# Every ninth weight unit of an expert layer moved as two transfers of 120 and 8 rows

## The reference

```python
for e in range(N_EXPERTS):
    y = y + combine[:, e:e + 1] * swiglu(xt, w_gate[e], w_up[e], w_down[e])
```

## Time and profile before

| | |
|---|---|
| time, median of 3 runs | 1594.76 us (1594.12 to 1596.35) |
| span of the profiled execution, first to last instruction | 1591.7 us |
| TensorE matmuls busy | 1517.8 us, 95% |
| TensorE weight loads busy | 1330.8 us, 84% |
| VectorE busy | 256.7 us, 16% |
| ScalarE busy | 179.0 us, 11% |
| data moved by DMA | 433.48 MB, mean 272 GB/s |
| reads from HBM | 428.89 MB |

### The profile page before, as it was taken

One profiled execution on the slowest core, in us unless ns is written; L12 is line 12 of the kernel. 1 busy time (PEld: TensorE's weight loads), 2 busy tenths in 40 slices (PEclk: granted clock), 3 DMA queues, 4 the chain that ended last, 5 costly groups with the idle time before them and its releaser, 6 DMA issues.

```text
span 1591.7 us, 54543 instructions
## 1 busy us (share of the span) xinstructions
PE 1517.8 (95%) x25973; PEld 1330.8 (84%) x25973; DVE 256.7 (16%) x489; ACT 179.0 (11%) x383; POOL 143.6 (9%) x167
## 2 busy tenths in 40 slices
PE   8999999999999999999999999999999999999997
PEld 7787587777687865989999999899999999998996
DVE  3433310000143435000010010010000000000102
ACT  3233120000131322100000000000000000000001
POOL 2243200000022532200000000000000000000000
PEclk9999999999999999999999999999999999999999
DMA  9213244444242245999999999999999999999992
GB/s 335 89 53 133 106 159 159 159 159 146 92 161 106 76 154 229 360 377 376 363 374 376 357 348 376 356 382 369 365 376 366 370 367 369 367 355 373 389 379 88
DMA packets 133612, 433.48 MB, mean 272 GB/s; under 512 B 9082, under 2 KB 33916, under 8 KB 119052
## 3 DMA queue, kind: packets, MB, share of 16 engines
q1 hardware_dynamic: 132384, 427.70, 71.9%
q0 software_dynamic: 672, 2.14, 0.4%
q10 hardware_dynamic: 332, 0.13, 0.0%
HBM read 428.89 MB, written 1.05 MB: 270 GB/s over the span
## 4 chain that ended last, share of the span: by engine, by line
PE 92%; issue 3%; DVE 2%; ACT 1%; POOL 1%; DMA 0%; ACTq 0%; DVEq 0%
PE ps L1133 35%; PE ps L1157 18%; PE ps L982 9%; PE ps L681 8%; PE ps L993 4%; PE ps L844 4%; PE ps L692 3%; PE ps L1190 2%; PE ps L1062 1%; PE ps L801 1%; PE ps L714 1%; PE ps L677 1%; PE ps L811 1%; PE ps L707 1%; PE ps L821 1%
## 5 line engine op out<-in xcount | busy, mean ns | idle before, releaser
L1157 PE MATMUL ps<-LT_sb,ring 128*64 128x88 f32 x5376 | 218.4, 239 | 16.2 <-issue 15.1
L1157 PEld LDWEIGHTS ps<-LT_sb,ring 128*64 128x64 f32 x5376 | 212.0, 137 | 21.7 <-issue 19.4
L1133 PE MATMUL ps<-wpost,ring 128*64 128x88 f32 x5376 | 217.0, 240 | 12.4 <-issue 10.9
L1133 PE MATMUL ps<-AT_sb,ring 128*64 128x88 f32 x5376 | 217.0, 239 | 9.9 <-issue 9.7
L1133 PEld LDWEIGHTS ps<-wpost,ring 128*64 128x64 f32 x5376 | 210.9, 138 | 17.5 <-issue 15.4
L1133 PEld LDWEIGHTS ps<-AT_sb,ring 128*64 128x64 f32 x5376 | 211.7, 138 | 14.6 <-issue 13.9
L982 PEld LDWEIGHTS ps<-hT_sb,ring 128*128 128x128 f32 x768 | 136.0, 190 | 24.6 <-issue 9.1
L982 PE MATMUL ps<-hT_sb,ring 128*128 128x256 f32 (+1 forms) x768 | 155.7, 362 | 0.0
L681 PE MATMUL ps<-hT_sb,ring 128*128 128x256 f32 x576 | 128.2, 380 | 0.0
L681 PEld LDWEIGHTS ps<-hT_sb,ring 128*128 128x128 f32 x576 | 108.1, 190 | 15.0 <-issue 0.5
L1985 POOL TENSOR_SCALAR small<-small 128x1 f32<-128x1 f32 x16 | 3.9, 241 | 1203.3 <-ACT late L1513 933.6
(11 more groups left out here) (284 smaller groups left out, 1156.5 us busy)
## 6 DMA issues: line engine op xcount, KB each, us to landing
ring<-in_moe_w_gate SPq DMA_DIRECT2D x84, 1024.0 KB, 8.4
ring<-in_moe_w_up SPq DMA_DIRECT2D x84, 1024.0 KB, 8.0
ring<-in_moe_w_down SPq DMA_DIRECT2D x84, 1024.0 KB, 8.2
late<-in_moe_w_up SPq DMA_DIRECT2D x28, 1024.0 KB, 8.5
late<-in_moe_w_gate SPq DMA_DIRECT2D x28, 1024.0 KB, 7.7
late<-in_moe_w_down SPq DMA_DIRECT2D x28, 1024.0 KB, 8.0
ring<-in_ffn_w_gate SPq DMA_DIRECT2D x11, 1024.0 KB, 5.4
ring<-in_ffn_w_up SPq DMA_DIRECT2D x11, 1024.0 KB, 8.1
```

Source lines behind the costliest of these rows:

```text
L1133: ins = mm(o[lo:lo + P // 2, :], pairs[:, m % 2, lo:lo + P // 2], xgT[e % 2][:, k, :], start=(k == 0 and m % 4 == 0), stop=(k == KD - 1), ...
L1157: ins = mm(o[lo:lo + P // 2, :], d[:, i, m * P + lo:m * P + lo + P // 2], moe_hid[:, 2 * j + i, :], start=(first and m % 4 == 0), stop=las ...
```

## The change

Every ninth unit (n mod 9 is 4) is loaded as two transfers, the partitions 0 to 119 and the partitions 120 to 127, into the same buffer and onto the same semaphore. Each of the two adds 16. What TensorE waits for is counted accordingly: 16 for each transfer that the buffer has had up to unit n.

```diff
+CUT_EVERY = 9
+CUTS = (0, 120, P)
+
+def rows_of(n):
+    return list(zip(CUTS, CUTS[1:])) if n % CUT_EVERY == CUT_EVERY // 2 else [(0, P)]
+
+def landings_through(n):
+    return 16 * sum(len(rows_of(m)) for m in range(n % N_UNIT, n + 1, N_UNIT))
...
-                    sp_.dma_start(dst, src).then_inc(unit_landed[n % N_UNIT], 16)
+                    for lo, hi in rows_of(n):
+                        sp_.dma_start(dst[lo:hi], src[lo:hi]).then_inc(unit_landed[n % N_UNIT], 16)
...
-                pe.wait_ge(unit_landed[n % N_UNIT], per_round(r, 16 * (n // N_UNIT + 1), 16 * ROUND_UNITS // N_UNIT))
+                pe.wait_ge(unit_landed[n % N_UNIT], per_round(r, landings_through(n), landings_through(ROUND_UNITS - N_UNIT + n % N_UNIT)))
```

## The result

The changed kernel takes 1714.7 us in the median (1704.23 to 1723.07, 4 runs), against 1594.44 us before (1590.05 to 1596.35, 4 runs): a ratio of 1.0761, 95% interval 1.0717 to 1.0804. It is slower by 120 us, where 28 us less were forecast. The span of the profiled execution is 1712.9 us, 121.2 us longer.

What follows compares the result with a forecast made beforehand. TensorE's matmul stream was taken as the bound, lengthened by 47.3 us of issue gaps from late program blocks. Issue and wait cost nothing; 60% of the gaps, 28 us, was gained: 1594.8 - 28 = 1567 us, range 1550 to 1605.

Steps and rivals of the forecast that it cites:

- What bounds the kernel: Expert layer, from 640 us: TensorE's matmul stream sets the end, lengthened by 47.3 us of issue gaps awaiting late program blocks.
- Program packets all on one engine: Expert layer: assumed all 170 program packets of q8 use one DMA engine, which then moves 23.7 MB against 20.9 MB.
- The sum of 25.9 GB/s: Expert layer: rate of one engine carrying its weights plus all program packets, put against a limit of 24.6 to 25.6 GB/s.
- The argument against evenly spread packets: Expert layer: spread evenly, each engine runs at 23.0 GB/s with 7 to 10% spare, so blocks would seldom be 1.6 us late.
- Bytes per engine: Cut units: 15 engines keep 8 rows each, the spared one loses 2.3 MB, eight engines gain 0.29 MB.
- The gain of 28 us: Expert layer: 60% of the 47.3 us of issue gaps disappears because program blocks arrive earlier on the spared engine.
- The cut transfer is slow: Rival, chance 0.11: cut units load slower, 1614 to 1640 us, or 1595 to 1610 in a milder form.
- 15 engines in each other's way: Milder form of the slow-transfer rival for cut units: the time ends between 1595 and 1610 us.
- 120 rows over 8 engines: Form of the slow-transfer rival: 15 rows per engine, 5.0 us instead of 2.7 per cut unit, 85 us more DMA time.
- third sign of being wrong: Expert layer: TensorE's issue gaps up by 10 us or more, meant to show program packets on one of the eight engines.
- program packets on one of the eight engines: Rival, chance 0.11: the fullest engine gets 0.30 MB more from the 8-row transfers, costing 11.7 us, 1606.5 us.
- SyncE's issue and the wait: Cut units: 37 more DMA starts, 14 us on SyncE but nothing on the path; waiting for 32 increments costs 0.

Runs made afterwards that it cites:

- f2: Kernel before, with the 37 units each loaded as eight transfers of 16 rows, one row on each of 16 engines: 1715.32 us, ratio 1.0778 to the kernel before.

## Why the prediction was wrong

*What bounds the kernel.* Right. TensorE's stream sets the end, issue gaps lengthen it, no matmul waits for a landing, and the gaps end 1.4 us behind a packet of program, in both kernels. The gaps grew when the rate fell.

*Program packets all on one engine.* Not borne out. The step that was looked for between 15 and 16 rows is not there, nor one between 8 and 15 beyond the bytes. The sum of 25.9 GB/s "at or over the limit" rested on this assumption alone and so was no evidence for it. The argument against evenly spread packets took the average load of an engine; that a block can queue behind a burst on any engine, at 23.0 GB/s too, fits the runs and is not shown by itself. Which engines carry the program stays open.

*Bytes per engine, the step that failed.* The count was right: 15 engines and 8, shown by 37 x 7 small packets. The rule for this number in the Trainium skill (DMA: Bandwidth & Descriptors, section Why a DMA increments its semaphore by 16 and not by 1) agrees; that they are the lowest-numbered engines is not shown by any run. What failed was to go from "8 rows each, as before" to the same speed. 8 rows on an engine take 303 ns per 4 KB in place of 164 once the transfer is not of all 128 rows, and what is in flight beside it slows with it.

*The gain of 28 us* therefore lost both of its supports: that the spared engine was the full one did not show, and the transfer that spared it made every packet in flight take nearly twice as long.

*The rivals.* "The cut transfer is slow" had the sign, the place and the test ("the loss per cut unit is over 0.8 us"). I gave it 0.11 and two forms. The form nearest to what was found, 15 engines in each other's way, I had priced at 1595 to 1610 us; it is 1714.7. The other, 120 rows over 8 engines, came near the size by a mechanism that isn't there. The reason that I set against this rival, that 8-row shares are what each engine does now, is the failed step again. A cut unit keeps the rate at half for 6 to 8 us, 1.4 MB (the cut unit and what runs beside it), about 3.5 us of lost engine time, and 121.2/37 = 3.3 us reach the end. That is not because DMA has no time to spare: the copies to HBM were added to the same kernel and cost 1.1 us each for 2.7 us of DMA time. Of the 3.3 us only 81.1/37 = 2.2 are gaps; the rest is the lower clock, which the shorter gaps of the copies did not bring. The prediction's third sign of being wrong, gaps up by 10 us or more, came true, but it was to point at program packets on one of the eight engines, and no run bears that out.

*The clock* was in no term at all. A third of the loss, 42 us, is matmuls at a lower clock. All 21 stretches at 1.2 GHz lie at gaps of 2.4 us and more, and the 101 gaps of up to 1.8 us with the copies of 120 rows brought none; yet 8 gaps of 2.3 to 3.6 us were not followed by one. No run kept TensorE busy through the gaps to show this share alone.

*SyncE's issue and the wait.* The cut by columns, with 37 more starts and the same two-transfer wait, cost about 14 us where nothing was forecast. The starts are not it, at 8 to 10 us for 320 of them, and pieces are smaller in the 11 down units among the 37 only (4 KB in place of 8, which is 11 x 128 = 1408 of the 2000 packets that its page has more; the others are the 592 small ones). What costs the 14 us stays open.

*Why fewer than 128 rows are slow* is settled as to place, not as to mechanism. It is on the write side of on-chip memory, with 15 engines and with 16, from 120 rows down to 16; 112 rows lose least. The Trainium skill (SBUF — State Buffer, section Door 1: The DMA port swizzle) describes 16 ports that DMA writes go through, each serving scattered groups of four partitions, and its page DMA: Bandwidth & Descriptors (section The descriptor swizzle) says that a 128-partition transfer gives each engine a port of its own. If each engine took a run of neighbouring rows instead, which no row here shows, that map would put two engines on a port. 303 against 164 ns at 120 rows agrees with this, and so do 190 to 229 GB/s at 64 rows. By the same account 16 rows lie on four ports and would go at a quarter; f2 shows half: its 349 packets of 4 KB from 1013 to 1021 us took 302 ns each. Eight such transfers in a row may drift over more ports, but no run shows that.

## What to carry to other kernels

A cut along the partitions is not neutral, even where each DMA engine keeps its number of rows: here transfers into on-chip memory of 120, 64, 32 and 16 rows about halved the rate of all that was in flight, and 112 rows cost 5.8%. Cut along the columns if a transfer must be cut: that cost 1.1%. And where DMA is at 97% and the program itself comes by DMA, TensorE can lose time to a slow load without ever waiting for its data: look for "issue" gaps at a fixed number of matmuls, and read the rate in slices of about a microsecond, since the average (368 to 327 GB/s) hides stretches at half.

## What the runs showed of the hardware

- A transfer of 120 rows ran on 15 engines and one of 8 rows on 8, by the count of small end packets. A transfer of one row of 8 KB was dealt to 16 engines in pieces of 512 B.
- 4 KB packets took 303 ns in place of 164 while a cut unit was in flight, at unchanged DMA share (0.97 to 0.99). Busy share says nothing of the rate.
- 37 copies from HBM to HBM showed no such loss: with 120 and with 128 rows of 8 KB they cost 2.65% and 2.58%.
- TensorE went on 1.4 us (median) after a 16 KB packet of queue q8 had landed, at 76 gaps of the changed kernel and 70 of the kernel before.
- The granted clock averaged 0.78 in the 6.5 us around and behind a gap of 2.51 us, and 64 matmuls took 4.22 us there; before, with gaps of 1.6 us at most, it stayed at 1.00 over the layer.
